# The order of small jobs, weight conversions and LRU blocks around a projection stream, on one core

## The reference

```python
# first block, each layer l
proj = h @ w_in[l]                       # hg columns, rw columns, gate columns
p_rw = token_shift(p_rw, rw_mu[l])
r, k, v, z_rw, w_down, a_down = split(p_rw)
w_raw = -softplus(-(rw_w0[l] + tanh(w_down) @ rw_w_up[l])) - 0.5
if l == 1:
    v_mix = sigmoid(rw_v0 + (h @ rw_v_down) @ rw_v_up)
    v = v + (v_first - v) * v_mix
a = sigmoid(rw_a0[l] + a_down @ rw_a_up[l])
kk = k * rw_k_k[l];  kk = kk / max(norm(kk), L2_EPS)     # per head
# second block, first layer
u = h @ w_in;  xb, gate = u[..., :1536], u[..., 1536:]
xb = causal_depthwise_conv(xb, conv_w, conv_b)           # 4 taps
r = sigmoid(blockdiag(xb, w_a) + b_a);  i = sigmoid(blockdiag(xb, w_x) + b_x)
log_a = -8 * r * softplus(-lam);  a = exp(log_a)
h_t = a_t * h_{t-1} + sqrt(1 - a_t**2) * i_t * xb_t
y = (h * silu(gate)) @ w_out
```

## Time and profile before

| | before |
|---|---|
| median of 3 runs | 2084.49 us (2082.9 to 2086.28) |
| time of the profiled execution | 2084.49 us, its span 2082.7 us |
| PE busy | 1896.6 us (91%) |
| DVE busy | 1003.1 us (48%) |
| ACT busy | 853.7 us (41%) |
| POOL busy | 694.2 us (33%) |
| mean granted TensorE clock | 0.975 |

### The profile page before, as it was taken

One profiled execution on the slowest core, in us unless ns is written; L12 is line 12 of the kernel. 1 busy time (PEld: TensorE's weight loads), 2 busy tenths in 40 slices (PEclk: granted clock), 3 DMA queues, 4 the chain that ended last, 5 costly groups with the idle time before them and its releaser, 6 DMA issues.

```text
span 2082.7 us, 35637 instructions
## 1 busy us (share of the span) xinstructions
PE 1896.6 (91%) x14368; PEld 1514.4 (73%) x14368; DVE 1003.1 (48%) x1327; ACT 853.7 (41%) x1219; POOL 694.2 (33%) x486
## 2 busy tenths in 40 slices
PE   3999988899997999988799997999989999998977
PEld 3777877699774777877699774676757877776755
DVE  6675476633545127576632635678625213132332
ACT  2343555533523444456433524355433223233332
POOL 2554532300242436522200341332524533242312
PEclk9999999999998999999999999999999999999998
DMA  8672221200422322222200523211233221121211
GB/s 324 238 235 80 86 91 66 81 4 4 162 91 84 124 81 76 97 76 74 72 4 4 182 91 114 108 61 51 94 118 112 91 81 61 61 71 51 71 61 71
DMA packets 60828, 192.92 MB, mean 93 GB/s; under 512 B 5632, under 2 KB 5888, under 8 KB 60320
## 3 DMA queue, kind: packets, MB, share of 16 engines
q1 hardware_dynamic: 60704, 191.10, 26.8%
HBM read 173.25 MB, written 17.83 MB: 92 GB/s over the span
## 4 chain that ended last, share of the span: by engine, by line
issue 49%; PE 22%; POOL 18%; DVE 4%; ACT 4%; DMA 1%; POOLq 0%; DVEq 0%; ACTq 0%; SPq 0%
POOL w_lo_sb L716 18%; PE proj L1977 11%; PE aux L2187 3%; DVE area_sb L1287 2%; DMA w_raw_sb<-wall 1%; PE aux L2118 1%; PE aux L2244 1%; PE proj L2187 1%; PE aux L2241 1%; DVE area_sb L1551 1%; ACT L813 1%; ACT w_hi_sb L793 0%; DVE area_sb L1290 0%; ACT stage_sb L937 0%; ACT L920 0%
## 5 line engine op out<-in xcount | busy, mean ns | idle before, releaser
L716 POOL TENSOR_TENSOR w_lo_sb<-w_raw_sb,w_hi_sb 128x512 fp32r<-128x512 f32 x462 | 676.0, 1484 | 1180.3 <-ACT w_hi_sb L793 1180.3
L1977 PE MATMUL proj<-act_hi_sb,w_hi_sb 128*128 128x512 f32 x1480 | 599.0, 405 | 19.4 <-POOL w_lo_sb L716 6.3
L1977 PE MATMUL proj<-act_hi_sb,w_lo_sb 128*128 128x512 f32 x1480 | 579.2, 391 | 0.0
L1977 PE MATMUL proj<-act_lo_sb,w_hi_sb 128*128 128x512 f32 x1480 | 578.5, 391 | 0.0
L793 ACT ACTIVATE w_hi_sb<-w_raw_sb 128x1024 fp32r<-128x1024 f32 x231 | 244.5, 1058 | 699.0 <-PE proj L1977 470.0
L1977 PEld LDWEIGHTS proj<-act_hi_sb,w_hi_sb 128*128 128x128 f32 x1480 | 279.6, 189 | 96.2 <-issue 28.2
L1977 PEld LDWEIGHTS proj<-act_lo_sb,w_hi_sb 128*128 128x128 f32 x1480 | 279.7, 189 | 61.1 <-issue 6.4
L1977 PEld LDWEIGHTS proj<-act_hi_sb,w_lo_sb 128*128 128x128 f32 x1480 | 279.1, 189 | 59.6
L1996 PE MATMUL aux<-act_hi_sb,w_hi_sb 128*128 128x512 f32 x336 | 137.5, 409 | 37.6 <-issue 23.4
L1287 DVE TENSOR_TENSOR area_sb<-area_sb 128x256 f32<-128x256 f32 (+2 forms) x208 | 140.8, 718 | 19.2 <-ACT area_sb L945 9.7
L1996 PE MATMUL aux<-act_lo_sb,w_hi_sb 128*128 128x512 f32 x336 | 134.4, 400 | 0.0
(11 more groups left out here) (251 smaller groups left out, 2544.8 us busy)
## 6 DMA issues: line engine op xcount, KB each, us to landing
w_raw_sb<-wall SPq DMA_DIRECT2D x231, 512.0 KB, 3.3
area_sb<-w_ada SPq DMA_DIRECT2D x32, 512.0 KB, 5.5
slots_sb<-w_ada SPq DMA_DIRECT2D x16, 512.0 KB, 8.1
gate_scr<-stage_sb SPq DMA_DIRECT2D x32, 256.0 KB, 2.2
area_sb<-gate_scr SPq DMA_DIRECT2D x8, 1024.0 KB, 9.1
x_scr<-area_sb SPq DMA_DIRECT2D x3, 2048.0 KB, 7.4
area_sb<-x_scr SPq DMA_DIRECT2D x3, 2048.0 KB, 10.6
area_sb<-lru_gates SPq DMA_DIRECT2D x1, 3584.0 KB, 13.3
```

Of the source, the lines that this page charges most:

```text
L716: nc.gpsimd.tensor_tensor(w_lo[:, b % 2, :, :].rearrange("p k n -> p (k n)")[:, half], w_raw[:, b % 2, half], w_hi[:, b % 2, :, :].rearran ...
L1977: ins = MM(bank, w[:, s, k, :], a[:, t, :], start=(start and i == 0), stop=(stop and i == len(terms) - 1))
```

## The change

It makes no difference to what is computed, only to three orders.

1. RWKV stage: all `w_up` and `a_up` products, and in layer 1 all `v_up` products, now run after the last K block and ahead of the V blocks, on PE and on ACT. The V and Z blocks become a loop of two turns of four blocks on both engines.
2. HGRN2 blocks, on ACT alone: the Exp of `norm_ready` comes straight after the Ln, with `keep(6)` behind it; `keep(7)` comes behind the Exp of the decays; `keep(9)` comes behind the last of the two Exps that follow `bn_ready`.
3. LRU stage: g blocks come later among the x blocks. Group 0 runs after 3 blocks instead of 6, group 1 after 9 instead of 10, groups 2 and 3 after 14 and 17 as before, but with x11 ahead of group 2. The lists of ACT and DVE follow.

```diff
@@ -35,8 +35,8 @@
 RET_LOG = [math.log(1.0 - 2.0 ** (-5.0 - h)) for h in range(RET_HEADS)]
 
 
-LRU_ORDER = [("x", 4), ("g", 0), ("g", 1), ("x", 5), ("g", 2), ("x", 6), ("g", 3), ("x", 7), ("g", 4), ("x", 8),
-             ("x", 9), ("g", 5), ("x", 10), ("g", 6), ("x", 11)] + [("g", j) for j in range(7, 12)]
+LRU_ORDER = [("x", 4), ("g", 0), ("x", 5), ("x", 6), ("g", 1), ("x", 7), ("g", 2), ("x", 8), ("g", 3), ("x", 9),
+             ("g", 4), ("x", 10), ("g", 5), ("x", 11)] + [("g", j) for j in range(6, 12)]
 
 
 def block_plan():
@@ -857,17 +857,19 @@
                     b += 1
                 for j in range(4):
                     scaled(b + j, 5 + j)
+                b += 4
                 for j in range(QT):
-                    scaled(b + 4 + j, 9 + j)
                     x = job_ready(act, ("w_up", l, j))
                     job_read(A(P1[:, j, :], x, ACT.Sigmoid, bias=V(f"w0{l}", j)), ("w_up", l, j))
                     x = job_ready(act, ("a_up", l, j))
                     job_read(A(P2[:, j, :], x, ACT.Sigmoid, bias=V(f"a0{l}", j)), ("a_up", l, j))
-                for j in range(QT):
-                    scaled(b + 8 + j, 13 + j)
-                    if l:
+                if l:
+                    for j in range(QT):
                         x = job_ready(act, ("v_up", l, j))
                         job_read(A(P3[:, j, :], x, ACT.Sigmoid, bias=V("v0", j)), ("v_up", l, j))
+                with act.Fori(0, 2) as turn:
+                    for j in range(4):
+                        scaled(b + j, 9 + j, turn)
                 evacuated(act, b_hg - 1)
                 evacuated(act, b_hg - 2)
                 A(P4, Z_, ACT.Sigmoid).then_inc(S("z_sig"), 1)
@@ -889,22 +891,21 @@
                 for j in range(QT):
                     evacuated_job(act, ("kk_sum", l, j))
                 chain.done(A(xa[:, 4:8, :], xa[:, 4:8, :], ACT.Ln, scale=2.0 ** 20))
-                keep(6)
                 A(xa[:, 4:8, :], xa[:, 4:8, :], ACT.Exp, scale=-0.5, bias=10.0 * math.log(2.0))\
                     .then_inc(S("norm_ready"), 1)
-                keep(7)
+                keep(6)
 
                 act.wait_ge(S("decay_ex"), l + 1)
                 A(P1, P1, ACT.Exp, scale=-RW_DECAY).then_inc(S("decay_exp"), 1)
                 if l == 0:
                     evacuated_job(act, ("ada", 1, 0))
+                keep(7)
                 keep(8)
 
                 act.wait_ge(S("bn_ready"), l + 1)
                 A(P2, P3, ACT.Exp, scale=RW_DECAY).then_inc(S("decay_in"), 1)
-                keep(9)
                 A(P3, P3, ACT.Exp, scale=-RW_DECAY).then_inc(S("decay_all"), 1)
-                for m in range(10, 12):
+                for m in range(9, 12):
                     keep(m)
                 for m in range(12, 16):
                     b = b_hg + m
@@ -1159,26 +1160,26 @@
 
             lru_block("x", 4)
             lru_block("g", 0)
+            lru_block("x", 5)
+            lru_rates(0)
+            lru_block("x", 6)
+            lru_decays(0)
             lru_block("g", 1)
-            lru_block("x", 5)
-            lru_block("g", 2)
-            lru_block("x", 6)
-            lru_rates(0)
-            lru_block("g", 3)
-            lru_decays(0)
             lru_block("x", 7)
             lru_roots(0)
-            lru_block("g", 4)
+            lru_block("g", 2)
             lru_block("x", 8)
+            lru_block("g", 3)
             lru_rates(1)
             lru_block("x", 9)
             lru_decays(1)
-            lru_block("g", 5)
+            lru_block("g", 4)
             lru_block("x", 10)
             lru_roots(1)
+            lru_block("g", 5)
+            lru_block("x", 11)
+            lru_rates(2)
             lru_block("g", 6)
-            lru_rates(2)
-            lru_block("x", 11)
             lru_decays(2)
             lru_block("g", 7)
             lru_roots(2)
@@ -1807,34 +1808,34 @@
 
             lru_block("x", 4)
             lru_block("g", 0)
+            lru_block("x", 5)
+            lru_inputs(0)
+            lru_block("x", 6)
+            lru_square(0, 0)
             lru_block("g", 1)
-            lru_block("x", 5)
-            lru_block("g", 2)
-            lru_block("x", 6)
-            lru_inputs(0)
-            lru_block("g", 3)
-            lru_square(0, 0)
             lru_square(0, 1)
             lru_square(0, 2)
             lru_block("x", 7)
             lru_scan(0, 0)
-            lru_block("g", 4)
             lru_scan(0, 1)
+            lru_block("g", 2)
             lru_scan(0, 2)
             lru_block("x", 8)
+            lru_block("g", 3)
             lru_inputs(1)
             lru_block("x", 9)
             lru_square(1, 0)
+            lru_block("g", 4)
             lru_square(1, 1)
-            lru_block("g", 5)
             lru_square(1, 2)
             lru_block("x", 10)
             lru_scan(1, 0)
             lru_scan(1, 1)
+            lru_block("g", 5)
+            lru_scan(1, 2)
+            lru_block("x", 11)
+            lru_inputs(2)
             lru_block("g", 6)
-            lru_scan(1, 2)
-            lru_inputs(2)
-            lru_block("x", 11)
             for o in range(3):
                 lru_square(2, o)
             lru_block("g", 7)
@@ -2054,23 +2055,22 @@
                     b += 1
                 for j in range(4):
                     used(project(b + j))
+                pe.wait_ge(S("tanh_done"), l + 1)
+                pe.wait_ge(S("up_in"), 16 + 32 * l)
                 for j in range(QT):
                     cols = slice(P * j, P * j + P)
-                    used(project(b + 4 + j))
-                    if j == 0:
-                        pe.wait_ge(S("tanh_done"), l + 1)
-                        pe.wait_ge(S("up_in"), 16 + 32 * l)
                     for name, q in (("w_up", slice(0, 64)), ("a_up", slice(64, 128))):
                         x = job_open(pe, (name, l, j))
                         job_full(MM(x, xa[q, 0, cols], wa[q, :], start=True, stop=True), (name, l, j))
-                for j in range(QT):
-                    cols = slice(P * j, P * j + P)
-                    used(project(b + 8 + j))
-                    if l:
-                        if j == 0:
-                            evacuated(pe, b_rw + 5)
+                if l:
+                    evacuated(pe, b_rw + 5)
+                    for j in range(QT):
                         x = job_open(pe, ("v_up", l, j))
-                        job_full(MM(x, xa[0:32, 2, cols], xa[0:32, 1, :], start=True, stop=True), ("v_up", l, j))
+                        job_full(MM(x, xa[0:32, 2, P * j:P * j + P], xa[0:32, 1, :], start=True, stop=True),
+                                 ("v_up", l, j))
+                with pe.Fori(0, 2) as turn:
+                    for j in range(4):
+                        used(project(b + 4 + j, turn=turn))
                 if l == 0:
 
                     pe.wait_ge(S("later_used"), KT)
@@ -2402,14 +2402,14 @@
                 for half, j in names:
                     used(project(lru_piece(half, j)))
 
-            lru_blocks(("x", 4), ("g", 0), ("g", 1), ("x", 5), ("g", 2), ("x", 6))
+            lru_blocks(("x", 4), ("g", 0), ("x", 5))
             pe.wait_ge(S("lru_w"), 16)
             lru_group(0)
-            lru_blocks(("g", 3), ("x", 7), ("g", 4), ("x", 8))
+            lru_blocks(("x", 6), ("g", 1), ("x", 7), ("g", 2), ("x", 8), ("g", 3))
             lru_group(1)
-            lru_blocks(("x", 9), ("g", 5), ("x", 10), ("g", 6))
+            lru_blocks(("x", 9), ("g", 4), ("x", 10), ("g", 5), ("x", 11))
             lru_group(2)
-            lru_blocks(("x", 11), ("g", 7), ("g", 8))
+            lru_blocks(("g", 6), ("g", 7), ("g", 8))
             lru_group(3)
             lru_blocks(("g", 9), ("g", 10), ("g", 11))
             side_by_side(("lru_out", 0), [(t + 8) % RT for t in range(RT)], fresh=SPLITS["lru_y"])
```

## The result

| | before | after |
|---|---|---|
| median of 4 runs | 2083.69 us (2077.86 to 2086.28) | 2109.93 us (2102.69 to 2115.07) |
| profiled execution, its span | 2084.49 us, 2082.7 us | 2106.91 us, 2105.1 us |
| mean granted TensorE clock | 0.975 | 0.969 |

After over before is 1.0111, with a 95% interval from 1.0090 to 1.0133: 23 us slower, above the range's upper end of 2105. All 26 runs of the changed kernel have a median of 2105.73 us, which fits this ratio; the four of the table lie a little higher. The profiles differ by 22.4 us.

What follows compares the result with a forecast made beforehand. PE was taken as the bound, busy 1896.6 of 2082.7 us, so each new PE wait is a loss. Terms 4.4 + 0 + 6.2 + 2.5 = 13.1 us on 2084.49 gave 2097.6 us, range 2088.5 to 2105.

Steps and rivals of the forecast that it cites:

- I add 1.6 to every new wait that is longer than the 2.56 us: PE's clock after long waits: 7 matmuls fewer in 3.4 us, 1.6 us per wait, estimated from one pair.
- step 1b: RWKV stage, layer 1: new sequence as long as the old, PE wait some 1.3 us; 0, between -0.5 and +0.8 us.
- 1a, layer 0: RWKV stage, layer 0: V blocks start 2.8 us later behind ACT's reads, plus 1.6 for the clock: +4.4 us.
- 2, hg8: HGRN2 blocks, layer 1: hg8's conversion behind the Exp starts hg8 4.6 us late, plus 1.6 for the clock: +6.2 us.
- 3, LRU: LRU stage: PE waits 4.8 us ahead of g3 for DVE's g2, plus 1.6 clock; net +2.5 us, between 0 and 8.
- The rivals: Shorter waits (2091.5 us, chance 0.14), DVE falls further behind (0.14), no measurable change (0.08), faster (0.04).
- DVE falls further behind: LRU stage: group 2 delayed too, a second wait of 5.5 us, 2103 us; chance 0.14.

Runs made afterwards that it cites:

- only part 1: Only the RWKV stage's new order (small products ahead of the V blocks, loops) applied to the kernel before: 2097.89 us, ratio 1.0091.
- the part alone: Only the new LRU order applied to the kernel before: 2086.82 us, ratio 1.0022.
- g2 first: Kernel before with only the new LRU order, and DVE's product of g2 moved ahead of group 0's first two scans: 2077.37 us, ratio 0.9966.

## Why the prediction was wrong

The direction was right, and so were the places, the releasers and the chains of all three new waits; the size, 13.1 us of 22.4 in the profile, was not.

*The step that failed* is "I add 1.6 to every new wait that is longer than the 2.56 us", with its other half in step 1b, "is below the length at which I saw the clock fall". It was one price and one threshold from one pair of rows, and the kernel then showed the lower level lasting from 3.4 to 13.7 us. The price is half of what part of the low stretch PE works through: 0.5 x (104.5 - 96.55) = 4.0 in layer 0, 0.5 x 13.7 = 6.8 in layer 1, 1.7 at hg8, 0.5 x (1391.3 - 1387.17) = 2.1 in the LRU stage. The sum is 14.6 us where I had 4.8. The missing 9.8 us are about what separates 13.1 from 22.4. PE's busy time says the same: 14.6, less the 1.7 us of low clock that only the kernel before has in the LRU stage, are 12.9, and PE was busy for 11.4 us more.

*1a, layer 0:* +4.4 against +8.9. The wait was 3.92 us (4.3), the clock cost 4.0 instead of 1.6, and PE had two more waits later, 1.05 for DVE and 1.31 for POOL, against "no further wait in the stage". Waits of that kind come and go between profiles: the kernel with only part 1 has 0.20 and 0.54 there.

*1b, layer 1:* 0 against +6.8. Worked through: K's end to V's start 14.35 us, less the 10.2 for eight inserts, plus half of the 5.2 us that V still runs at the lower level, is 6.8. The ACT chain was right (wait 1.59 for 1.3). The loops cost nothing, as assumed: V's start to the norm's sums is 67.96 us for twelve blocks, and less those 2.6 us it is 12 x 5.45. The four `v_up` at "1.06 to 0.8 each" took 1.8 each. Two groups were tried by themselves: the eight 64-row products with their wait (+3.2 in the stretch) and the run of 32-row products (+1.7), and removing both took the low clock away. That it is the wait in the first group is likely, not shown: taking it out also made a run of eight products into one of six and one of two. How the stretches at the lower level join, and why together they cost 6.7, more than both, the runs don't tell.

*2, hg8:* +6.2 against +5.4. hg8 was to be late by 4.6 us and is by 4.84 (it starts 7.87 us after the `rk_sum` products ahead of it, 3.03 before); the clock took 1.7. 1.1 us of it were given back up to the first head, with part 1 and without. The Exp had its own table load of 1.28 us behind the Ln, as in the earlier trace rows. By the Trainium skill, ScalarE: Activation LUTs, "Table sets: the hidden batching unit", that load wouldn't be there and the sum would be 4.9; the measurement decides for the load.

*3, LRU:* +2.5 against +2.5, +4.3 for the part alone: right in total, and by errors that cancel. The wait was 7.09, not 4.8: PE came 1.3 us earlier and DVE 0.9 later. PE was earlier because no low clock follows on the wait ahead of x5 in this profile; I had called the block at 1314.14 x5 "as before", but in the kernel before the third block is g1. That missing 1.7 us is also most of the difference to the +4.3 of the part alone, so that the total met the forecast is luck. DVE took 27.1 us for what I had put at 25.0: it holds ten operations that last 0.6 to 1.1 us longer than their like, as 1.13 against 0.54 and 1.77 against 0.68, one for each of POOL's ten halves of five blocks. I had counted fewer of them. After it all four later waits but one vanished, 3.3 us in sum, more than the half that I had expected.

*The rivals.* None of them was it. "DVE falls further behind" named the right place for the larger wait, but no second wait came. By the Trainium skill, SBUF — State Buffer, "SBUF: two separate sides", the one of DVE and GpSimd that starts first holds their port pair for its whole instruction and the other "fully blocks". I had made of this the loss of a whole POOL operation each time; here DVE loses 0.6 to 1.1 us by such pairs of rows, while POOL's halves last 1.4 to 1.7 us in this stretch. That doesn't contradict the page, since an operation that comes late into POOL's would only lose the rest of it; the runs don't show which it is.

What no rival held is a clock that stays down for two to four times as long.

## What to carry to other kernels

Grouping small matmuls is no saving by itself. Behind a short wait among matmuls of few rows, or behind a run of them, the clock stood at the lower level for up to 13.7 us here and cost up to 6.8 us, more than the start-ups that the grouping saves. Price a clock drop by its whole length in more than one place of the profile, not by one pair. And where engines work in order, look for the cure of a wait for a bank at the engine that reads it: moving one product of DVE ahead of two scans turned +0.22% into -0.34%.

## What the runs showed of the hardware

- Four `v_up` products of 32 rows in a row, with PE never idle, were followed by the lower clock level (20 matmuls in 6.8 us); with 128 rows of other operands, same count and width, not (32 in 6.8 us; one profile of each). Six products of 64 rows without a wait were not.
- A wait of 1.59 us among 64-row products was followed by a low clock; before, 1.34 us ahead of 128-row blocks was not the earlier trace rows.
- A wait of the same length isn't always followed by the same clock. Ahead of the LRU stage's third block PE waits 2.56 us in every kernel here: ahead of g1 in the kernel before, ahead of x5 in the changed one and in the one with g2 first. In the last two the low clock of the earlier trace rows is missing: 15 matmuls in the 3.4 us behind the wait. PE's row, then the window, of the kernel with g2 first (part 3 alone):

```profile
1314.82 0.47 PE L1977 MATMUL proj<-act_hi_sb,w_hi_sb 128*128 128x512 f32 x1 [2.56 <-ACT stage_sb L1124]
```
```profile
1314.82:1318.20 3.38, 3.38 (x15) 2.79 (x16) 3.27 (x4) 0.81 (x1) 2.78 (x3) 1.00 0.48 155
```
- For that reason the profiles of kernels that share a stage can differ in it by a microsecond or two, so a term below 2 us is better judged by the timed ratio or by a wait's row than by the span.
